# The last attention block worked by head pairs, its steps set between the projection matmuls

## The reference, cut to what matters

```python
def _rms(x, g):
    y = xf * lax.rsqrt(jnp.mean(xf * xf, axis=-1, keepdims=True) + EPS)
    return y.astype(x.dtype) * g
def _heads(h, w, g=None):
    t = (h @ w).reshape(b, n, -1, HEAD_DIM)
    return t if g is None else _rms(t, g)
...
        s_loc = jnp.einsum('bwhd,brwchd->bhwrc', q_r, k_win) * scale + bias
        s_ctx = jnp.einsum('bwhd,bnhd->bhwn', q_r, k_ctx) * scale
        p = jax.nn.softmax(jnp.concatenate([s_loc, s_ctx], axis=-1), axis=-1)
        return einsum(p_loc, v_win) + einsum(p_ctx, v_ctx)
```

## Time and profile before

| | |
|---|---|
| median of 3 runs | 3105.3 us (3100.55 to 3109.58) |
| the profiled execution's own time | 3100.61 us |
| its span, first to last instruction | 3098.8 us |
| PE busy | 2885.5 us (93%) |
| DVE, ACT, POOL busy | 1626.7, 1133.8, 1090.1 us |
| mean granted TensorE clock | 0.966 of full |

### The profile page before, as it was taken

How to read it: one execution, slowest core, us unless ns; L and a number is a source line. 1 busy time by engine, 2 the same in 40 slices (tenths; PEclk the granted TensorE clock), 3 DMA queues, 4 the chain that set the end, 5 groups by cost and what they waited for, 6 DMA issues and landing times.

```text
span 3098.8 us, 39305 instructions
## 1 busy us (share of the span) xinstructions
PE 2885.5 (93%) x14018; PEld 2347.0 (76%) x14018; DVE 1626.7 (52%) x2371; ACT 1133.8 (37%) x1857; POOL 1090.1 (35%) x501
## 2 busy tenths in 40 slices
PE   4998899998998899997999799999979989989999
PEld 3885588886776578874878688888858878868887
DVE  6537696854456788855222416655542565431111
ACT  3333443334464533235112413121243357542222
POOL 2440444445322444443212123232323233234443
PEclk9999899998999899998999899999979989999999
DMA  5351355532421355531211123333312110122222
GB/s 209 122 181 34 119 187 203 190 109 79 158 69 65 108 185 193 178 109 42 68 68 48 41 82 115 130 133 121 126 61 67 50 42 22 36 76 98 95 95 88
DMA packets 90419, 325.47 MB, mean 105 GB/s; under 512 B 10036, under 2 KB 12852, under 8 KB 89784
## 3 DMA queue, kind: packets, MB, share of 16 engines
q1 hardware_dynamic: 85392, 312.21, 29.5%
q10 hardware_dynamic: 4904, 11.68, 1.2%
HBM read 321.75 MB, written 2.10 MB: 105 GB/s over the span
## 4 chain that ended last, share of the span: by engine, by line
PE 84%; DVE 8%; ACT 4%; issue 2%; DMA 1%; POOL 1%; DVEq 0%; ACTq 0%; SPq 0%; POOLq 0%
PE bank L1293 58%; PE junk L1295 9%; PE bank L1076 2%; PE bank L1221 2%; PE bank L1061 1%; PE bank L1208 1%; PE bank L1310 1%; PE bank L1200 1%; PE bank L1180 1%; PE junk L1200 1%; ACT UF L816 1%; ACT Uh L816 1%; PE bank L1102 1%; DVE ADA L1383 1%; DMA ADA<-in_ast 1%
## 5 line engine op out<-in xcount | busy, mean ns | idle before, releaser
L466 POOL TENSOR_TENSOR WL<-RAW,WH 128x1024 fp32r<-128x1024 f32 x392 | 979.1, 2499 | 1784.4 <-ACT WH L760 1276.7
L760 ACT ACTIVATE WH<-RAW 128x1024 fp32r<-128x1024 f32 x292 | 307.2, 1052 | 381.9 <-PE junk L1295 188.1
L1293 PE MATMUL bank<-U1h,WH 128*128 128x512 f32 x960 | 378.1, 394 | 18.0 <-DVE U1l L1631 17.8
L1293 PE MATMUL bank<-Uh,WH 128*128 128x512 f32 x832 | 341.2, 410 | 55.5 <-DVE Ul L1633 54.9
L1293 PE MATMUL bank<-U1l,WH 128*128 128x512 f32 x960 | 375.5, 391 | 0.0
L1293 PE MATMUL bank<-U1h,WL 128*128 128x512 f32 x960 | 375.4, 391 | 0.0
L1293 PE MATMUL bank<-Hh,WH 128*128 128x512 f32 x864 | 340.2, 394 | 11.7 <-DVE Hl L548 11.7
L1293 PE MATMUL bank<-Hl,WH 128*128 128x512 f32 x864 | 339.0, 392 | 0.0
L1293 PE MATMUL bank<-Hh,WL 128*128 128x512 f32 x864 | 338.8, 392 | 0.0
L1293 PE MATMUL bank<-Ul,WH 128*128 128x512 f32 x832 | 331.5, 398 | 0.0
L1293 PE MATMUL bank<-Uh,WL 128*128 128x512 f32 x832 | 331.2, 398 | 0.0
(11 more groups left out here) (334 smaller groups left out, 5249.3 us busy)
## 6 DMA issues: line engine op xcount, KB each, us to landing
RAW<-in_wst SPq DMA_DIRECT2D x392, 512.0 KB, 3.4
ADA<-in_ast SPq DMA_DIRECT2D x192, 512.0 KB, 4.5
NST<-in_nstrip ACTq DMA_DIRECT2D x16, 192.0 KB, 2.3
XT<-in_xt SPq DMA_DIRECT2D x1, 2048.0 KB, 15.4
STRIP<-in_strip ACTq DMA_DIRECT2D x8, 256.0 KB, 2.6
CB<-in_cb ACTq DMA_DIRECT2D x4, 512.0 KB, 4.2
DX<-in_dx ACTq DMA_DIRECT2D x1, 2048.0 KB, 8.3
out_xt<-XT SPq DMA_DIRECT2D x1, 2048.0 KB, 6.2
```

The source lines that it names most:

```text
L466: pool.tensor_tensor(WL[:, s4], RAW[:, s2], WH[:, s4].bitcast(F32), ALU.subtract)\
L760: act.activation(WH[:, c % 4], RAW[:, c % 2], ACT.Copy).then_inc(S("hi_done"), 1)
L1293: mm = pe.matmul(bank_of(p, u)[:], w[:, u, k], x[:, k, 0:T], start=st and m == 0, stop=en and m == 2)
```

## The change

The three projection phases become one, `nakqv`, of 24 jobs in the order key, query, value of each head pair (tile t). In tile 0 all three jobs run together, one k at a time, into banks 0, 1 and 3, with the context in banks 2 and 6. In tile 1 the key and query jobs run alone, and the value job's eight units (one k of one job) lie between the first eight attention steps, which are those of tile 0. From there on each attention step has three units between its parts, for the tile after the one that attention is at. In the last eight steps the units are those of the first four `res2` jobs.

The scores of a step go as three matmuls of 512 columns into one bank (context and local keys lie side by side), and DVE takes bias, sum and maximum in one instruction. `av` has 64 moving columns; the four products of a head lie in one bank, and DVE takes them out together (`store`). The norm's inverse root is exp(-0.5 ln x) on ACT with one Newton step on DVE, in buffers of its own for queries and keys; keys are scaled first, and the query's mean square (`query_ms`) waits for the scaled key, since both use bank 4. PTN and the banks of scores and transposes are single.

```diff
-    add("na_q", 8, 3, "u", 48)
-    add("na_k", 8, 3, "u", 48, ctx=True)
-    add("na_v", 8, 3, "u", 48, ctx=True)
+    add("nakqv", 24, 3, "u", 48)
...
+            def neighbourhood_pool():
...
+                for u in range(3):
+                    lo(N_J0 + u, u, u % 2)
+                pool.wait_ge(S("ada_done"), NADA)
+                pool.memset(NB[:, 0:256], 0.0).then_inc(S("nbias_done"), 1)
+                lo(N_J0 + 3, 3, 1)
+                lo(N_J0 + 4, 0, 0)
+                pool.wait_ge(S("nmask_land"), 16)
+                key_lo(0)
+                bias(0)
+                query_lo(0)
+                lo(N_J0 + 5, 1, 1)
+                for t in range(1, KT + 1):
+                    bias(2 * t - 1)
+                    lo(N_J0 + 3 * t + 3, (3 * t + 3) % 4, (3 * t + 3) % 2)
...
+            def neighbourhood_act():
...
+                def turned(n):
+                    act.wait_ge(S("n_turned"), n + 1)
+                    if n >= 1:
+                        act.wait_ge(S("n_av"), n)
+                    act.activation(PTN[:], BANK[5][:], ACT.Copy).then_inc(S("n_pt"), 1)
...
+                round_hi(N_J0 + 3, 3)
+                key_out(0)
+                act.dma_start(NMK[:], a["nmask"]).then_inc(S("nmask_land"), 16)
+                for h in range(2):
+                    load_nstrip(act, h)
+                act.preload_act_table_set("natural_log_exp_and_others")
+                query_out(0)
+                round_hi(N_J0 + 4, 0)
+                value_out(0)
+                key_root(0)
+                query_root(0)
+                key_hi(0)
+                round_hi(N_J0 + 5, 1)
+                key_out(1)
+                query_hi(0)
+                for n in range(N_N + 2):
+                    t, s = n // 8 + 1, n % 8
+                    if s == 0 and 2 <= t <= KT:
+                        value_out(t - 1)
+                    if 1 <= n <= N_N:
+                        numerators(n - 1)
...
+                    if s == 5 and t < KT:
+                        query_out(t)
+                        key_root(t)
+                    if s == 6 and t < KT:
+                        key_hi(t)
+                        round_hi(N_J0 + 3 * t + 5, (3 * t + 5) % 4)
+                    if s == 7 and t < KT:
+                        query_root(t)
+                    if n >= 2:
+                        turned(n - 2)
...
+            def job(t, c, ks):
+                j = N_J0 + 3 * t + c
+                main = (0, 1, 3)[c] if t == 0 else j % 2
+                ctx = 6 if t == 0 and c == 2 else 2
+                for k in ks:
+                    if k == 0:
+                        pe.wait_ge(S("lo_done"), j + 1)
+                        if t >= 1:
+                            pe.wait_ge(S("bank_read"), j if c == 0 and t >= 2 else j - 1)
...
+            def query_ms(t):
+                pe.wait_ge(S("n_qsq"), t + 1)
+                pe.wait_ge(S("n_scaled"), 2 * t + 1)
+                pe.matmul(BANK[4][:], HALF[:], QSQ[:, t % 2], start=True, stop=True).then_inc(S("n_qms"), 1)
...
+            def turn(n):
+                pe.wait_ge(S("n_exp"), n + 1)
+                if n >= 1:
+                    pe.wait_ge(S("n_pt"), n)
...
+                for q, tile in enumerate((7, 8, v0, v1)):
+                    mm = pe.matmul(BANK[6][:, b * NHD:(b + 1) * NHD], PTN[:, q * P:(q + 1) * P], VN[:, t % 2, tile, i * NHD:(i + 1) * NHD],
+                                   start=q == 0, stop=q == 3)
...
+            for k in range(KT):
+                pe.wait_ge(S("u_ready"), 48 + k + 1)
+                for c in range(3):
+                    job(0, c, (k,))
+            for unit in range(3):
+                stream_part(1, unit)
+            key_ms(0)
+            for unit in range(3, 11):
+                stream_part(1, unit)
+            query_ms(0)
+            for unit in range(11, 16):
+                stream_part(1, unit)
+            for n in range(N_N + 3):
+                t, s = n // 8 + 1, n % 8
+                if t == 1:
+                    units = ((16 + s,), (), ())
+                elif t < KT:
+                    units = ((3 * s,), (3 * s + 1,), (3 * s + 2,))
...
+                if s == 0 and t >= 2:
+                    if n < N_N + 2:
+                        turn(n - 2)
+                    av(n - 3)
...
+                def root(t, query):
...
+                    link(dve.tensor_tensor(NRT[:, 0:w], y, y, ALU.mult))
...
+                    link(dve.scalar_tensor_tensor(out=NRT[:, 0:w], in0=NRT[:, 0:w], scalar=-3.0, in1=y,
+                                                  op0=ALU.add, op1=ALU.mult))
```

More of the change, by code:

```diff
@@ L325, in banks_of @@
                 return (0, 1, 2, 3)
+            if p["kind"] == "res2" and p["layer"] == 3:
+                return (0, 1, 2, 4)
             return (0, 1, 4, 7) if p["layer"] < 2 else (0, 1)
@@ L347, in peeled, with na_keys, two @@
         def peeled(p):
-            return p["j0"] == 0 or (p["seen"] == 0 and p["kind"] in ("v", "up", "na_k", "na_v", "res"))
+            return p["j0"] == 0 or (p["seen"] == 0 and p["kind"] in ("v", "up", "res"))
         def first(p, kind, layer):
             return p["kind"] == kind and p["layer"] == layer and not (p.get("group") or 0)
-        NA_J_END = next((p["j0"] for p in PHASES if first(p, "res2", 3)))
+        N_J0 = next(p["j0"] for p in PHASES if p["kind"] == "nakqv")
+        N_RES = N_J0 + 24
+        N_N = NH * 4
+        NA_LOC = slice(C, TC)
+        def na_keys(t, b):
+            return slice(t % 2 * TC, t % 2 * TC + 2 * (C + NA_KEY0[b]))
+        def two(ap):
+            return ap.rearrange("p (a n) -> p a n", a=2)[:, :, 0:256]
         hb = sqb = yb = gates = 0
@@ new lines, in scores @@
+            def scores(n):
+                h, b = divmod(n, 4)
+                t, i = h // 2, h % 2
+                r, q = slice(64 * i, 64 * i + 64), slice(b * P, (b + 1) * P)
+                if n % 8 == 0:
+                    pe.wait_ge(S("n_lo"), 2 * t + 2)
+                if n == 0:
+                    pe.wait_ge(S("bank_read"), N_J0 + 3)
+                else:
+                    pe.wait_ge(S("n_z"), n)
+                keys = na_keys(t, b)
+                passes = ((QNh[r, t % 2, q], KNh), (QNh[r, t % 2, q], KNl), (QNl[r, t % 2, q], KNh))
+                for m, (w, x) in enumerate(passes):
+                    mm = pe.matmul(two(BANK[3][:]), w, two(x[r, keys]), start=m == 0, stop=m == 2)
+                mm.then_inc(S("n_score"), 1)
@@ new lines, in neighbourhood_pe @@
+            query_ms(0)
[7 more added lines that the diff above has]
+                    units = ((3 * s,), (3 * s + 1,), (3 * s + 2,))
+                else:
+                    units = ((), (), ())
+                if s == 0 and t >= 2:
+                    if n < N_N + 2:
+                        turn(n - 2)
+                    av(n - 3)
+                for unit in units[0]:
+                    stream_part(t, unit)
+                if t == KT and s < 6:
+                    residual((s,), (0,))
+                elif t == KT:
+                    residual((0, 1) if s == 6 else (4,), (3,))
+                if 2 <= n < N_N + 2 and s:
+                    turn(n - 2)
+                for unit in units[1]:
+                    stream_part(t, unit)
+                if t == KT and s < 6:
+                    residual((s,), (1,))
+                elif t == KT:
+                    residual((2,) if s == 6 else (5,), (3,))
+                elif n == N_N + 1:
+                    residual((6,), (0, 1))
+                if t < KT and s == 4:
+                    key_ms(t)
+                if t < KT and s == 6:
+                    query_ms(t)
+                if 2 <= t <= KT and s == 6:
+                    turn_back(t - 2)
+                if n < N_N and s:
+                    scores(n)
+                for unit in units[2]:
+                    stream_part(t, unit)
+                if t == KT and s < 6:
+                    residual((s,), (2,))
+                elif n == N_N - 2:
+                    residual((3,), (3,))
+                elif n == N_N + 2:
+                    residual((6,), (2, 3))
+                if n < N_N and not s:
+                    scores(n)
+                if n >= 3 and s:
+                    av(n - 3)
+                if t <= KT and s < 3:
+                    value_turn(t - 1, s)
```

521 lines of the change are left out of this document (270 added, 251 removed).

## The result

The changed kernel takes 3136.2 us (median of 4 runs, 3131.8 to 3141.6), the kernel before 3107.4 beside it (4 runs, 3100.6 to 3110.9): a ratio of 1.0095, 95% interval 1.0068 to 1.0123. It is slower, by some 29 us where plus 16 was forecast.

The account below looks back on a forecast made before the run. PE was taken to bound the stage. Terms summed to 454.7 us, plus 3 for half clock: 457.7 against 440.5, plus 17; on the 3105.3 median that gives 3122, stated as 3121, range 3096 to 3142.

Parts of the forecast that it names:

- the fill: Tile 0's three projection jobs, sharing each k, keep PE busy: 24.6 us, 2.5 of it until the clock rises.
- wait at F: At the end of the fill, PE idles 3.8 us until ACT's query copy frees a bank for tile 1's key job.
- to unit 15: Tile 1's key and query units with `key_ms` and `query_ms`, before its value job's wait: 18.8 us, 2.5 for the clock.
- wait for weights: In tile 1's value job, PE idles 6.8 us for weights whose low part stands behind other work on POOL.
- tile 1's steps: The first eight attention steps, with one unit each: 33.6 us, including waits of 4.5 and half clock of 2.3.
- six full tiles: Six tiles of eight attention steps with interleaved projection units: 48.5 us each, 2.1 of it waits; 291 in all.
- the end: `res2`, the last eight attention steps, tails, values and turning back: 76.1 us, 6.3 of it waits.
- the root chain: From the end of s = 4 through ACT and DVE to `query_ms`: 9.4 us; PE waits 1.4 in each tile.
- the third rival: Single buffers bite more: each step's `turn` waits 0.3 for PTN, low clock in each tile; 22 us more, 3143; chance 0.18.
- `av` at 64 columns: Attention's value products: the weight load sets their pace, 0.11 us a record, so halving the moving columns gains nothing.
- the first rival: In attention, `av` halves because moving columns set its pace: 28 us go, giving 3094, faster; chance 0.13.
- the second rival: The two waits at the start are shorter, tile waits don't touch the clock: about plus 6, 3111; chance 0.24.

Follow-up runs that it names:

- the start order: The changed kernel with ACT's three transfer issues and the table load moved behind the first value copy: 3135.3 us, 1.0074 of the kernel before.
- earlier weights: The changed kernel with unit 15's weights rounded by ACT right behind the value copy and split by POOL before the key's low part: 3126.6 us, ratio to before 1.0057.
- earlier roots: The changed kernel with the key's root on ACT and DVE in step 4 instead of step 5: 3119.9 us, 1.0036 of the kernel before.
- the four edits: The changed kernel with earlier roots, earlier weights, the start order and a second PTN buffer together: 3094.3 us, 0.9944 of the kernel before.

## Why the prediction was right, and where its sum was off

The direction, slower, and the range held: the stage was forecast at 457.7 and took 468.1, so 17.2 of the 27.6 us of loss were foreseen. By its terms (us):

| term | forecast | measured | shown by |
|---|---|---|---|
| the fill | 24.6 | 24.6 | windows |
| wait at F | 3.8 | 3.6 | released by QN; halved by the start order |
| to unit 15 | 18.8 | 17.8 | windows |
| wait for weights | 6.8 | 7.2 | released by WL; 3.5, behind QNl, with the earlier round |
| tile 1's steps | 33.6 | 41.6 | half clock |
| six full tiles | 291 | 292.6 | windows |
| the end | 76.1 | 80.7 | wait at L1500, 3.3; half clock, 3.4 us long |
| half clock in the tiles | 3 | none of its own | clock at 1.00 |

**The step that failed in size is tile 1's.** The forecast put its waits at 4.5 and its half clock at 2.3. The waits were 4.2. At half clock PE ran the first 12.5 us, which costs about half of that, and again for 8.7 us beside the wait of 3.18: together 10.6, so 8.3 over. These idle stretches and their releasers were right; how long half clock stays after them was taken from the one row of a short idle in dense projection work. The stretch around the 7.2 us of idle lasted 17.1 us (12.5 of it behind the idle), the one at the 3.18 us wait, with 1.0 of idle just ahead of it, 10.2, and with the earlier weights the one behind 3.5 us 3.4: the length of the idle alone doesn't give it. The runs with earlier roots and earlier weights each took a part of it away.

**The end** missed a wait. The second four `res2` jobs need the four buffers that the first four, interleaved, hold to their end; POOL had been idle 46.8 us before that round, and PE waited 3.28 for it:

```profile
2739.39 2.35 POOL L482 TENSOR_TENSOR WL<-RAW,WH 128x1024 fp32r<-128x1024 f32 x1 [46.76 <-ACT WH L666]
```

With the half-clock stretch of 3.4 us, about 1.7 by half its length, that covers the 4.6.

**The full tiles agree by two errors that cancel.** Without its waits the forecast's tile is 48.5 - 2.1 = 46.4; the tile that the four edits leave is 45.1. The waits were 3.7, not 2.1: the key root at nearly 1.5 where 1.4 stood, and PTN at 2.4 where 0.75 stood (0.25 of that counted in both). The work was 1.3 less: over a step an `av` takes 0.82 up to what follows it, not 0.98, and a turn 0.37, not 0.50, against scores of 0.89, not 0.78. The sum of the root chain is also 9.3 by its own terms, not 9.4. So the third rival (0.18), that the single buffers bite more, was half right: its 22 us are nearly the 20.2 measured, but most comes from one turn a tile and what it delays; only three steps of eight lose its 0.3, and the clock has no part in it but at the end. A tile that comes out right says little about the terms in it.

**`av` at 64 columns** was taken at 0.11 a record and measured at 0.11, with 128 columns the same: the first rival is excluded. (The transposes' loads that spoke for it start 0.06 apart, where the forecast had 0.07 from their total.) With the rule of the Trainium skill that the prediction gives ("TensorE: Matmul & The Clock Gate", section LDWEIGHTS), 107 ns for a load of 128 columns, the trace agrees at full clock. At half clock, in the run with 64 columns before, it doesn't: 0.22 each.

**The second rival** (shorter waits at the start) is excluded: both had nearly the forecast's length.

**Two of the signs failed.** The stages before 2285 did not stand still: the stage began 10.2 us later, by the pace of the execution. And `res2` ended at 2763.9, not near 2743, by that and by the 10.4 us missing in the sum.

DVE's work in the stage fell from 209.9 to 152.7. That this bought nothing, as the forecast has it, was argued and not tried alone.

The forecast never asked what the change is worth with its waits taken away. By the four edits together that is 16.4 us; the change lost it, and 27.6 more, to four orders and buffers. Which part of it the fill gives and which the denser tiles wasn't tried alone.

## What to carry to other kernels

When two streams of work are woven on one engine, price every single buffer and every queue order at the weave: the list of waits put the one-buffer wait at 0.84 us a tile, and taking it away gave 2.4, since a wait delays the engine that releases the next one. Charge a wait with the half clock behind it, read from the clock column, since busy time doesn't show it. If a woven stage comes out slower, take its waits away one by one before giving it up; here the four added up, and turned plus 0.95% into minus 0.56%.

## What the runs showed of the hardware

Halving the columns of a product whose pace didn't hang on them at full clock saved nothing and cost 106 us in a stage that starts at half clock: PE stayed at half for 286.7 us, 47.8 with half of the products full again, 20.5 with all of them (30.7 with all of them and one PTN buffer). What else could bring the clock back there was not tried.

The full-clock pace of pairs of 512 and 256 columns is not one number: 2310 or 2265 matmuls in 400 us for the same program, 2% apart. Why an execution gets one or the other stays open.

A DVE pass took 2.40 us beside POOL instead of 0.69. This is the root of a query in the kernel with all four edits (timeline), where the scores then wait 1.9 us for the query's low part, the end of this chain:

```profile
2372.37 2.39 POOL L482 TENSOR_TENSOR WL<-RAW,WH 128x1024 fp32r<-128x1024 f32 x1
...
2372.90 2.40 DVE L2002 TENSOR_TENSOR NRT<-QSQ 128x512 f32<-128x512 f32 x1
2375.34 0.75 DVE L2004 SCALAR_TENSOR_TENSOR NRT<-bank,PRM,NRT 128x512 f32<-128x512 f32 x1
...
2600.91 0.69 DVE L2002 TENSOR_TENSOR NRT<-QSQ 128x512 f32<-128x512 f32 x1
```

The same pass takes 0.69 us in a later tile with POOL idle, and here 2.40: it ended 0.5 after POOL's pass. It is the only one of the eight such passes of this run that is so long. The Trainium skill ("SBUF — State Buffer", section "SBUF: two separate sides") says that a VectorE operation with two SBUF inputs and a GpSimd operation that reads SBUF exclude each other for the whole instruction, and these rows agree.
